# Hybrid decoder layer (FoX attention | RWKV-7 | top-4-of-32 MoE): an identity loaded early, and small matrix products issued in pairs on the four quarters of the array

## What is computed

```python
h = rmsnorm(x, mix_norm[i])
z = h @ w_in[i]                       # 1024 x (2056 + 1792)
# RWKV-7 group, 8 heads of 64, a state S (value x key) per head:
state = (state * w_t[:, :, None, :] + sa[..., None] * b_t[:, :, None, :]
         + v_t[..., None] * k_t[:, :, None, :])       # sa = state @ a_t
y_t = einsum('bhvk,bhk->bhv', state, r_t)
# FoX group, 8 heads of 64: causal softmax(q k / 8 + c[t] - c[s]) v, c = cumsum(log f)
x = x + concat([fox_out, rwkv_out]) @ w_out[i]
x = x + moe_ffn(rmsnorm(x, moe_norm[i]), ...)         # top-4 of 32, 12 MB of weights per expert
x = x + sigmoid(rmsnorm(x, ple_norm[i]) @ w_ple_gate[i]) * (p[i] @ w_ple_proj[i])
return rmsnorm(x, final_norm)
```

## Time and profile before

| | |
|---|---|
| median of 3 runs | 1221.32 us |
| profiled execution | 1219.11 us |
| its span | 1217.3 us |
| mean granted clock of PE | 0.996 |
| PE busy | 1154.9 us, 95% |
| PE weight loads busy | 496.8 us, 41% |
| DVE busy | 283.2 us, 23% |
| ACT busy | 170.7 us, 14% |
| read from HBM | 433.31 MB, 357 GB/s over the span |

### The profile page before, as it was taken

One profiled execution on the slowest core, in us unless ns is written; L12 is line 12 of the kernel. 1 busy time (PEld: TensorE's weight loads), 2 busy tenths in 40 slices (PEclk: granted clock), 3 DMA queues, 4 the chain that ended last, 5 costly groups with the idle time before them and its releaser, 6 DMA issues.

```text
span 1217.3 us, 16496 instructions
## 1 busy us (share of the span) xinstructions
PE 1154.9 (95%) x6852; PEld 496.8 (41%) x6852; DVE 283.2 (23%) x576; ACT 170.7 (14%) x317; POOL 0.2 (0%) x4
## 2 busy tenths in 40 slices
PE   6999998999999999999999999999999999999997
PEld 5888867443333333323333333333333333332334
DVE  2442625331211211111111111111111111111123
ACT  2321324120010000000010000000000000000114
POOL 0000000000000000000000000000000000000000
PEclk9999999989999999999999999999999999999999
DMA  9731023659999999999999999999999999999970
GB/s 381 301 139 70 3 96 106 234 233 384 430 427 428 428 429 428 429 428 429 428 429 428 428 429 430 427 427 430 430 427 427 430 429 425 430 430 427 425 317 34
DMA packets 32226, 434.87 MB, mean 357 GB/s; under 512 B 3968, under 2 KB 4096, under 8 KB 5824
## 3 DMA queue, kind: packets, MB, share of 16 engines
q1 hardware_dynamic: 32192, 434.37, 85.0%
HBM read 433.31 MB, written 1.05 MB: 357 GB/s over the span
## 4 chain that ended last, share of the span: by engine, by line
DMA 42%; PE 39%; ACT 0%; DVE 0%; issue 0%; SPq 0%; DVEq 0%
DMA ring<-in_we 42%; PE PS L836 27%; PE PS L921 2%; PE PS L684 2%; PE PS L798 2%; PE PS L813 2%; PE PS L850 1%; PE PS L805 1%; DMA hT<-in_wproj 1%; PE PS L734 0%; PE PS L880 0%; PE PS L860 0%; PE PS L740 0%; PE PS L493 0%; PE PS L821 0%
## 5 line engine op out<-in xcount | busy, mean ns | idle before, releaser
L836 PE MATMUL PS<-ring,FV 128*64 128x512 f32 x2304 | 515.5, 596 | 26.0 <-DMA ring<-in_we 26.0
L836 PEld LDWEIGHTS PS<-ring,FV 128*64 128x64 f32 x2304 | 158.0, 137 | 364.5 <-issue 302.1
L836 PE MATMUL PS<-B,FV 128*64 128x512 f32 x768 | 174.0, 596 | 9.4 <-DMA B<-in_we 8.7
L836 PEld LDWEIGHTS PS<-B,FV 128*64 128x64 f32 x768 | 53.0, 137 | 114.4 <-issue 98.7
L481 PE MATMUL PS<-hT,ring 128*128 128x256 f32 x416 | 93.6, 382 | 1.1 <-ACT hT L974 1.1
L481 PEld LDWEIGHTS PS<-hT,ring 128*128 128x128 f32 x416 | 78.1, 190 | 12.9 <-ACT hT L974 1.3
L1455 DVE TENSOR_SCALAR rz<-con,lora 64x64 f32<-64x64 f32 x30 | 7.4, 246 | 306.1 <-PE PS L836 306.1
L1537 DVE TENSOR_SCALAR hT<-PS 128x512 f32<-128x512 f32 x32 | 22.1, 691 | 185.6 <-PE PS L836 185.6
L1229 DVE TENSOR_TENSOR FV<-PS,prm 128x512 f32<-128x512 f32 x32 | 22.1, 691 | 184.0 <-PE PS L805 184.0
L798 PE MATMUL PS<-xq,rz 128*64 128x512 f32 x256 | 62.0, 605 | 0.0
L813 PE MATMUL PS<-B,rz 64*128 64x512 f32 x248 | 61.6, 615 | 0.0
(11 more groups left out here) (262 smaller groups left out, 657.4 us busy)
## 6 DMA issues: line engine op xcount, KB each, us to landing
ring<-in_we SPq DMA_DIRECT2D x144, 2048.0 KB, 24.2
B<-in_we SPq DMA_DIRECT2D x48, 2048.0 KB, 29.3
ring<-in_wz SPq DMA_DIRECT2D x7, 2048.0 KB, 22.5
ring<-in_wo SPq DMA_DIRECT2D x2, 2048.0 KB, 8.1
ring<-in_wgate SPq DMA_DIRECT2D x2, 2048.0 KB, 38.7
con<-in_con SPq DMA_DIRECT2D x1, 1053.0 KB, 7.0
xq<-in_x SPq DMA_DIRECT2D x2, 512.0 KB, 4.4
ring<-in_wz SPq DMA_DIRECT2D x1, 1024.0 KB, 9.5
```

Of the source, the lines that this page charges most:

```text
L836: mm = pe.matmul(PS[64 * h:64 * h + 64, bank_, :], lhs(4 * (q % 2) + k), w[:, k, h, :], start=(first and k == 0), stop=(q % 2 == 1 and k = ...
```

## The change

1. **Identity early.** `ident` moves from `con` to `prm` (now 197 columns); SP loads x's first half, `prm`, x's second half, `wz0`, `wz1`, then `con` and the small weights. DVE no longer scales x: it scales the identity by 1/rms (128x128 per half), and PE multiplies x by that in place of the transposes.
2. **Sets in pairs.** `per_head` takes several products and issues, for each g, both halves of each. A product marked `turned` writes the other half of PSUM than the one its operands stand in. Paired are: the two halves of `ma0`; `aa0` with its transpose (which DVE masked out of tile 9 before); `t{k}` with `tt{k}`; `q1` with `kp0`, `q2` with `vp0`, `q3` with the first half of `mk0` and `q5` with the second. `vp0`, `kp0` and `mk0` as steps of their own are gone.
3. **Order.** The masked matrix goes to `lora`. The fillers move: `z22` before `q1`, `z26` after it, `z23` to level 5, `z28` behind `d0`. `first_item(0)` goes after `z23`.

```diff
-MIX_ORDER = [("z", 18), ("bp", 0), ("z", 19), ("kp", 0), ("z", 20), ("ma", 0), ("z", 21), ("mk", 0),
-             ("z", 22), ("aa", 0), ("z", 26), ("zh", 23), ("q", 1), ("z", 23), ("qsq", 0), ("ffa", 0), ("ffe", 0),
-             ("t", 1), ("tt", 1), ("fc", 0), ("qss", 0), ("q", 2), ("qexp", 0), ("zh", 24), ("t", 2), ("tt", 2), ("qn", 0),
-             ("z", 24), ("q", 3), ("zh", 25), ("t", 3), ("tt", 3), ("kss", 0), ("q", 4), ("kexp", 0), ("z", 25), ("fg", 0),
-             ("t", 4), ("tt", 4), ("kn", 0), ("zh", 27), ("q", 5), ("z", 27), ("tt", 5), ("zh", 28), ("z", 28)]
-MIX_ORDER += [("x", 0), ("sc", 0), ("u", 0), ("sc", 1), ("d", 0), ("y", 0)]
+MIX_ORDER = [("z", 18), ("bp", 0), ("z", 19), ("ma", 0), ("z", 20), ("aa", 0), ("z", 21), ("z", 22),
+             ("q", 1), ("z", 26), ("qsq", 0), ("ffa", 0), ("ffe", 0), ("t", 1), ("fc", 0), ("qss", 0),
+             ("q", 2), ("qexp", 0), ("zh", 24), ("t", 2), ("qn", 0), ("z", 24), ("q", 3), ("zh", 25), ("t", 3), ("z", 25),
+             ("q", 4), ("kss", 0), ("kexp", 0), ("t", 4), ("kn", 0), ("zh", 23), ("q", 5), ("z", 23), ("fg", 0), ("tt", 5),
+             ("zh", 27), ("z", 27)]
+MIX_ORDER += [("x", 0), ("sc", 0), ("u", 0), ("sc", 1), ("d", 0), ("zh", 28), ("z", 28), ("y", 0)]
...
             for b in range(TB):
+                pe.wait_ge(s_x[b], 16)
                 pe.wait_ge(s_dve, dve_at[f"hn{b}"])
                 for k in range(KD):
-                    mm = pe.transpose(PS[:, k, b * P:(b + 1) * P], hn[:, b, k * P:(k + 1) * P], ident)
+                    mm = pe.matmul(PS[:, k, b * P:(b + 1) * P], xs[:, b, k * P:(k + 1) * P], scale_x[b], start=True, stop=True)
...
+            def per_head(*products, n=CH):
 
                 for g in range(16):
-                    for h2 in range(2):
-                        rows = slice(64 * h2, 64 * h2 + 64)
-                        f = PSF[rows, b0 * 512 + g * n:b0 * 512 + (g + 1) * n]
-                        mm = pe.matmul(f, lhs(rows, g), rhs(rows, g), start=True, stop=True)
+                    for b0, lhs, rhs, turned in products:
+                        for h2 in range(2):
+                            f = PSF[half(h2 ^ turned), b0 * 512 + g * n:b0 * 512 + (g + 1) * n]
+                            mm = pe.matmul(f, lhs(half(h2), g), rhs(half(h2), g), start=True, stop=True)
                 return mm
...
-                    fin(per_head(4, blocks(4), ar, 2 * CH), "ma0")
+                    fin(per_head((4, blocks(4), ar(0), 1), (6, blocks(4), ar(1), 0)), "ma0")
...
-                    fin(per_head(4, lambda rows, g: AR[rows, g, 0, :], blocks(4)), "aa0")
+                    fin(per_head((4, ar(0), blocks(4), 1), (6, blocks(4), ar(0), 0)), "aa0")
...
                 if kind == "q":
-                    pe.wait_ge(s_dve, dve_at[f"tt{k - 1}" if k > 1 else "mq1"])
-                    fin(per_head(4, blocks(1), blocks(8)), f"q{k}")
+                    pe.wait_ge(s_dve, dve_at[f"mq{k}"])
+                    if k > 1:
+                        pe.wait_ge(s_dve, dve_at[f"t{k - 1}"])
+                    beside = ()
+                    if k == 1:
+                        beside = ((4, blocks(1), eye, 0),)
+                    elif k == 2:
+                        pe.wait_ge(s_act, act_at[f"z{NZ}"])
+                        beside = ((2, blocks(2), eye, 0),)
+                    elif k == 3:
+                        pe.wait_ge(s_act, act_at["vp"])
+                        beside = ((2, blocks(1), ar(0), 0),)
+                    elif k == 5:
+                        pe.wait_ge(s_act, act_at[f"z{NZ - 1}"])
+                        beside = ((0, blocks(1), ar(1), 0),)
+                    fin(per_head((6, masked, blocks(8), 1), *beside), f"q{k}")
                 elif kind == "t":
                     pe.wait_ge(s_act, act_at[f"q{k}"])
-                    fin(per_head(6, blocks(14), blocks(4)), f"t{k}")
+                    if k > 1:
+                        pe.wait_ge(s_dve, dve_at[f"tt{k - 1}"])
+                    else:
+                        pe.wait_ge(s_act, act_at["kp"])
+                    fin(per_head((6, blocks(14), blocks(4), 1), (4, blocks(4), blocks(14), 0)), f"t{k}")
...
                     pe_done(f"q{n}")
-                    fin(act.activation(flat(4), two(4), ACT.Copy), f"q{n}")
+                    fin(act.activation(flat(4), two(6), ACT.Copy), f"q{n}")
+                    if n == 1:
+                        fin(act.activation(flat(7), two(4), ACT.Copy), "kp")
+                    elif n == 2:
+                        fin(act.activation(flat(3), two(2), ACT.Copy), "vp")
...
-                fin(v.tensor_scalar(hn[:, b, :], xs[:, b, :], col[:, 4 + b:5 + b], None, ALU.mult), f"hn{b}")
-            v.wait_ge(s_in, 32)
+                v.wait_ge(s_prm, 16)
+                fin(v.tensor_scalar(scale_x[b], ident, col[:, 4 + b:5 + b], None, ALU.mult), f"hn{b}")
```

More of the change, by code:

```diff
@@ L93 @@
 PE_STEPS = ([f"hT{k}" for k in range(KD)] + ["z0", "z1"] + [f"z{n}" for n in range(2, 7)] + ["uwua"]
-            + [f"z{n}" for n in range(7, 10)] + ["g", "ssk"] + [f"z{n}" for n in range(10, 16)] + ["vp0", "z16", "z17", "bn"])
+            + [f"z{n}" for n in range(7, 10)] + ["g", "ssk"] + [f"z{n}" for n in range(10, 18)] + ["bn"])
 PE_STEPS += [f"{kind}{n}" for kind, n in MIX_ORDER if kind not in ASIDE]
@@ L180, in p_ @@
             return prm[:, a:a + 1]
+        ident = prm[:, PARAM["ident"][0]:PARAM["ident"][1]]
         def flat(i):
@@ L202, in fox_rwkv7_moe_ple @@
         KT = xq[:, D:2 * D].rearrange("p (j t) -> p j t", j=NJ)
-        hn = B[:, PLACE[0]:PLACE[0] + 2, :]
+        scale_x = [B[:, PLACE[b], 0:P] for b in range(TB)]
         AR = B[:, PLACE[10]:PLACE[10] + 2, :].rearrange("p a n -> p (a n)").rearrange("p (g s c) -> p g s c", g=16, s=2)
@@ L316, in _ @@
         def _(sp):
-            for b in range(TB):
-                sp.dma_start(xs[:, b, :], t["x"][:, b * D:(b + 1) * D]).then_inc(s_x[b], 16)
-            sp.dma_start(con[:, :], t["con"]).then_inc(s_in, 16)
-            sp.dma_start(prm[:, :], t["prm"]).then_inc(s_in, 16)
+            sp.dma_start(xs[:, 0, :], t["x"][:, 0:D]).then_inc(s_x[0], 16)
+            sp.dma_start(prm[:, :], t["prm"]).then_inc(s_prm, 16)
+            sp.dma_start(xs[:, 1, :], t["x"][:, D:2 * D]).then_inc(s_x[1], 16)
             def piece(n, src, cols):
@@ L532, in _ @@
             for n in range(10, 18):
-                if n == 16:
-                    pe.wait_ge(s_dve, dve_at["sh13"])
-                    pe.wait_ge(s_act, act_at["g"])
-                    fin(per_head(4, blocks(2), eye), "vp0")
                 z(n)
@@ L634, in both @@
                             for h2 in range(2):
-                                rows = slice(64 * h2, 64 * h2 + 64)
+                                rows = half(h2)
                                 mm = pe.matmul(PSF[rows, at + j * 64:at + (j + 1) * 64], lhs(rows, g, j), rhs(rows, g, j),
@@ L1022, in _ @@
                 z(n)
-            act.wait_ge(s_dve, dve_at["tildes"])
-            pe_done("vp0")
-            fin(act.activation(flat(3), two(4), ACT.Copy), "vp")
             def rsqrt(dst, src, eps_col):
@@ L1347, in _ @@
                     mask_level(1)
[L1348 to L1354 removed]
+                elif kind == "q":
+                    if n < 5:
+                        mask_level(n + 1)
+                    if n == 3:
+                        fin(tt(b16(2), banks16(2), bc("strictT"), ALU.mult), "mks")
+                    elif n == 5:
+                        pe_done("q5")
+                        fin(tt(b16(13), banks16(0), bc("inclT"), ALU.mult), "mki")
+                elif kind in ("t", "tt"):
+                    pe_done(f"{kind}{n}")
+                    if kind == "t":
+                        fin(tt(flat(8), two(6), flat(8), ALU.add), f"t{n}")
                     fin(tt(flat(14), two(4), flat(14), ALU.add), f"tt{n}")
@@ L1680 @@
     prm[0:NHEAD, PARAM["fb"][0]] = a["fox_f_bias"][0]
+    prm[:, PARAM["ident"][0]:PARAM["ident"][1]] = np.eye(P)
     w_in = a["w_in"][0]
```

98 lines of the change are left out of this document (43 added, 55 removed).

## The result

The changed kernel takes 1200.3 us (median of 4 runs, 1198.85 to 1202.45) where the kernel before took 1221.3 us on the same chip (4 runs, 1220.86 to 1221.45): ratio 0.9832, 95% interval 0.9817 to 0.9847, or 21 us less. Its profiled execution took 1198.85 us, with a span of 1197.1 us at a mean granted clock of 0.997.

The account below looks back on a forecast made before the run. PE's own time bounds the path to the first load by a used expert piece, transfers the rest. Terms -16.7 - 0.8 - 0.7 - 0.2 - 0.3 + 0.5 = -18.2 us gave 1203.1 us; own range 1200.5 to 1206, full range to 1212.

Parts of the forecast that it names:

- A paired set costs 2.0 us: PE's paired sets: 64 matmuls, 128 records on all four quarters, take 2.0 us, against 3.88 us for two separate sets.
- The argument from L850: Four matmuls, two row groups by two column halves, take 1.01 us, so 3.5 of 4 run at once.
- the rival of a rate limit: PE's record starts limit paired sets: about 1212 us with some gain (chance 0.13), about 1221.7 with none (0.05).
- My 3.2 us: A paired set's time by the skill's floor: 128 records at 25 ns each, kernel about 1215 us.
- The sum over the sets, -16.7 us: PE's steps removed or paired, over 10 paired sets, save 16.7 us together.
- The start, -0.8 us: PE begins at about 6.7 us with doubled records; projections start at 13.4 instead of 14.21 us (+0.2 to -1.4).
- The waits: PE's waits in the new order: -0.7 us and -0.2 us for waits covered by `z` blocks, +0.5 us before `z24`.
- the 0.71 us: PE's wait in the first level, forecast to go because `z21` and `z22` cover DVE's five operations behind `aa0`.
- The slack of 0.1 us at `q4`: DVE finishes `t3`'s first addition at 25.6 us, PE wants `q4` at 25.7; DVE-queue rival: about 1206 to 1208, chance 0.08.
- Nothing behind the first used piece matters, and the end follows: From SP's first load waiting for a used expert piece, transfers run without pause; shortening PE's path there shortens the kernel equally.
- The clock, 2 us either way: Granted clock falls to 0.57 at 248 us behind the router's small matmuls; this can fall otherwise, 2 us either way.
- The slower rival: Paired sets: straight-to-turned steps empty the array, 1.9 us more per set on top of 3.88, 1241 us; chance 0.04.

Follow-up runs that it names:

- e1: Changed kernel with the two products of each pair issued one after the other instead of alternating; 1216.22 us, ratio 0.9969 to the kernel before.
- e2: Changed kernel with all products straight, none turned, still alternating, so only two of four quarters work; 1218.0 us, ratio 0.9976 to the kernel before.
- e5: Changed kernel with only the four pairs of t and tt issued in turn, all others alternating; 1206.3 us, ratio 0.9885 to the kernel before.
- e4: Changed kernel with the identity early, but DVE scaling x, 16 transposes kept and x's second half ahead of `prm`; 1198.65 us, ratio 0.9823.
- e10: Changed kernel with the router's products streaming w_router's 32 columns four times over, into 128 columns; 1198.21 us, ratio 0.9823 to the kernel before.

## Why the prediction was right

**The forecast, 1203.1 us**, stands 2.8 above the median, which lies 0.2 under the low end of my range, 1200.5; by the ratio (0.9832 of 1221.32) it is 1200.8, just inside. On the profiled executions, where the sum was made, it was 1200.9 against 1198.85; the other 0.8 us is that I took the median 2.2 us above the profiled execution, and it is 1.45. By its steps:

- **A paired set costs 2.0 us:** 2.02 measured. The argument from L850, four quarters at once in a burst, held for 128 records; the rival of a rate limit is out at this length. It is not out in general: behind 190 to 208 records PE did stop. The Trainium skill's floor of some 25 ns between starts of matmuls ("TensorE: Matmul & The Clock Gate", section "Wait — 56ns, not 53.3ns?") does not hold here from one quarter to the next: records of two different products start within 20 ns of each other. My 3.2 us from it counted records; a product stands as two, and per product the set's mean is 31.6 ns, which that floor would have allowed.
- **The sum over the sets, -16.7 us:** e1, e2 and e5 give it back, 1.69 us per set when in turn and 1.86 when straight; ten sets straight cost 17.6 us by the ratios, four in turn 6.5.
- **The start, -0.8 us:** this was the wrong term; it is +0.1 (14.29 us against 14.21). PE began at 7.25 instead of 6.7, and the 32 records took 6.47 us, 202 ns each, the slow end of my two (10.1 + 3.4 + 0.9 = 14.4, measured 14.29). I had both ends and took a value between them, though the only row of this stretch, the 16 transposes at 213 ns, was a slow one. Doubling the records in a slow stretch was the edit's price, and it ate what the early identity brought; e4 shows the 2.4 us that it hid.
- **The waits:** the 0.71 us is gone, `zh24` waits 0.28 instead of 0.5. The slack of 0.1 us at `q4` was enough: PE did not wait for DVE in the levels, and DVE's queue was walked right (`t3`'s additions took DVE from 132.25 us on, 2.48 us for the two, so the first ended near 133.5; `q4` began at 133.62). By these the sum up to the state steps was -17.4 without the start, and -18.0 came out (-17.94 with the start's +0.1); of the 0.6 us, 0.2 is `zh24`, and the rest isn't assigned.
- **Nothing behind the first used piece matters, and the end follows:** 19.62 us there, 20.2 in the span. It follows to within the spread of that part, 951.65 to 953.3 us in twelve of thirteen profiles; the 0.6 us here are of that size. I had forecast 247 us for that piece; it came at 245.38, because of the next point.
- **The clock, 2 us either way:** this was in my own range, and it is most of the 1.68 us that the router's part gave. That the profiled execution got the shorter fall was luck, for the forecast had no reason for it: other executions of the changed kernel have a mean clock of 0.995. e10 shows that the fall also hangs on the width of the router's products, and that an edit can take it away.
- **The slower rival**, that a turned quarter empties the array, is out: at 15.8 ns per record there is no place for it.

So the mechanism and the main term were right. On the profiled execution the start was off by 0.9 us up, the sets with their waits by 0.6 down, the router's part by 1.7 down and the part behind the first used piece by 0.6 down: together the 2 us. Had the clock and the last part been as before, the sum would have been met to 0.3 us, because the first two nearly cancel.

## What to carry to other kernels

Small products that leave quarters of the array idle are worth pairing, if the pair's records alternate in the program and between them use all four quarters; either alone gives almost nothing, and a measured burst of four such records was enough to forecast it. A matmul that saves another engine's step is no gain where PE is slow or already the one waited for: count its records at the price of their stretch. And when runs of one kernel spread over several microseconds, read the granted clock behind its narrowest products, and count PE's records in the first 20 us, where the clock column stayed at 1.00 at half the rate, before judging any edit of that size.

## What the runs showed of the hardware that was not expected

- Products in turn overlap only at their seam, by a few records (rows 112.35 to 112.47 us above): PE looks past a busy quarter, but not far.
- Behind some 200 records at 15.7 ns PE stops by itself for 0.86 to 1.15 us, four times in four.
- Four times the columns in the router's products cost 0.08 us per 16 records and kept the granted clock of that part at 1.00: a mean clock of 0.998 or more in ten of ten executions, against 8 of 43 with the narrow ones.
- The end of PE's slow start moved from about 12.9 us to about 18.2 us between two executions (changed kernel, and the one with the old start), and the granted clock in the profile's rows said 1.00 throughout.
- Each quarter took a new record every 0.06 us, with two quarters at work as with four; with all four, starts of different products stood less than 0.01 us apart (0.02 us for four).
- The small load of `prm` ahead of x's second half makes ACT wait 1.25 us for that half, which without it came in time.
